# The first refill of the expert ring sent in two transfers behind the first chunk, and output weights laid out by column halves

## The reference

```python
def hier_moe(h, w_rg, b_rg, w_re, b_re, w_gate, w_up, w_down):
    ...
    for e in range(N_EXPERTS):
        hid = jax.nn.silu(t @ w_gate[e]) * (t @ w_up[e])
        out = out + gates[:, e:e + 1] * (hid @ w_down[e]).astype(f32)
```

## Time and profile before

| | |
|---|---|
| median of three runs | 704.38 us (703.09, 704.38, 705.97) |
| profiled execution, its own time | 704.35 us |
| its span, first to last instruction | 702.5 us |
| mean granted TensorE clock | 0.971 of full speed |
| TensorE busy | 636.7 us |
| DMA | 234.09 MB, mean 333 GB/s |
| attention (layer 0's mixer) | about 0 to 155 us |
| experts of layer 0 | about 155 to 355 us |
| gated linear attention | about 355 to 500 us |
| experts of layer 1 | about 500 to 702 us |

### The profile page before, as it was taken

How to read it: one execution, slowest core, us unless ns; L and a number is a source line. 1 busy time by engine, 2 the same in 40 slices (tenths; PEclk the granted TensorE clock), 3 DMA queues, 4 the chain that set the end, 5 groups by cost and what they waited for, 6 DMA issues and landing times.

```text
span 702.5 us, 11653 instructions
## 1 busy us (share of the span) xinstructions
PE 636.7 (91%) x5189; PEld 381.3 (54%) x5189; DVE 234.0 (33%) x509; ACT 130.4 (19%) x287; POOL 44.2 (6%) x69
## 2 busy tenths in 40 slices
PE   7999999999999979959799999999999996778686
PEld 6654875467556635525378544645665552534433
DVE  2137863154332323203145701312723332123122
ACT  2145762111101100100122412222221100001001
POOL 1033100000000000000020600000000000000000
PEclk9999999999999989989999999999999998899899
DMA  9900583739999999999995505559599999999996
GB/s 351 387 37 1 237 363 140 340 120 371 435 428 433 421 437 424 430 433 420 428 424 220 239 1 240 239 221 376 241 383 440 424 420 443 415 437 429 427 423 253
DMA packets 13415, 234.09 MB, mean 333 GB/s; under 512 B 1712, under 2 KB 2864, under 8 KB 3760
## 3 DMA queue, kind: packets, MB, share of 16 engines
q1 hardware_dynamic: 12944, 233.09, 79.1%
q10 hardware_dynamic: 416, 0.18, 0.1%
HBM read 232.22 MB, written 1.05 MB: 332 GB/s over the span
## 4 chain that ended last, share of the span: by engine, by line
PE 62%; DMA 33%; DVE 2%; ACT 1%; issue 1%; SPq 0%; POOL 0%
DMA mem<-in_experts 25%; PE ps L1032 9%; PE ps L717 8%; PE ps L1244 8%; DMA rows<-in_experts 7%; PE ps L781 5%; PE ps L870 4%; PE ps L1235 4%; PE ps L1046 3%; PE ps L1073 3%; PE ps L818 3%; PE ps L808 1%; PE ps L774 1%; DMA mem<-in_mla_w_in 1%; PE ps L890 1%; PE ps L903 1%
## 5 line engine op out<-in xcount | busy, mean ns | idle before, releaser
L1032 PE MATMUL ps<-mem,hT 128*32 128x256 f32 x1824 | 112.4, 400 | 32.7 <-DMA mem<-in_experts 32.6
L1032 PEld LDWEIGHTS ps<-mem,hT 128*32 128x32 f32 x1824 | 60.7, 115 | 84.7 <-DMA mem<-in_experts 39.9
L781 PE MATMUL ps<-mem,rows 128*128 128x128 f32 x512 | 68.0, 292 | 6.3 <-issue 5.0
L781 PEld LDWEIGHTS ps<-mem,rows 128*128 128x128 f32 x512 | 63.2, 203 | 11.2 <-issue 9.5
L717 PE MATMUL ps<-mem,hT 128*128 128x512 f32 x128 | 57.3, 598 | 1.1 <-ACT hT L1592 1.1
L1046 PE MATMUL ps<-mem 128*32 128x512 f32 x464 | 53.1, 595 | 5.4 <-DMA mem<-in_experts 3.4
L1965 DVE TENSOR_TENSOR rows<-rows,ps 128x512 f32<-128x512 f32 x60 | 40.7, 686 | 48.6 <-PE ps L1073 48.4
L1073 PE MATMUL ps<-hT,mem 128*128 128x512 f32 x120 | 55.7, 606 | 0.6 <-ACT hT L1517 0.6
L1244 PE MATMUL ps<-mem,hT 128*128 128x512 f32 x128 | 55.8, 594 | 0.0
L1509 ACT ACTIVATE mem<-ps 128x256 f32<-128x256 f32 x16 | 9.9, 616 | 217.7 <-PE ps L1032 217.7
L1955 DVE TENSOR_TENSOR mem<-mem,ps 128x256 f32<-128x256 f32 x16 | 9.7, 607 | 116.6 <-ACT mem L1509 116.6
(11 more groups left out here) (331 smaller groups left out, 681.6 us busy)
## 6 DMA issues: line engine op xcount, KB each, us to landing
mem<-in_experts SPq DMA_DIRECT2D x31, 4096.0 KB, 33.2
mem<-in_experts SPq DMA_DIRECT2D x25, 2048.0 KB, 22.5
rows<-in_experts SPq DMA_DIRECT2D x9, 2048.0 KB, 29.9
mem<-in_gla_parts SPq DMA_DIRECT2D x3, 4096.0 KB, 27.4
mem<-in_mla_o SPq DMA_DIRECT2D x1, 4096.0 KB, 30.9
mem<-in_gla_parts SPq DMA_DIRECT2D x2, 2048.0 KB, 47.8
mem<-in_mla_w_in SPq DMA_DIRECT2D x2, 1344.0 KB, 9.5
mem<-in_mla_uq SPq DMA_DIRECT2D x1, 2304.0 KB, 15.8
```

Source lines behind the costliest of these rows:

```text
L781: mm = pe.matmul(spot(k), xn[:, i, k, :], Sg[:, i, :], start=first and k % HK == 0, stop=not first, skip_group_check=True)
L1032: mm = pe.matmul(ps[32 * j:32 * j + 32, 2, m * FE:(m + 1) * FE], xe[:, k, 32 * j:32 * j + 32], w[:, j, c * FE:(c + 1) * FE], start=k == 0 ...
```

## The change

Three things are done together.

1. The output weights of both mixers are laid out by column halves, `(b k n)` for `(k n)`: columns 0 to 511 of all chunks, then columns 512 to 1023. Each column half is exactly one place of the ring. In layer 0 half 8 is then issued at out_done 7 and half 9 at out_done 8; in layer 1 half 9 at out_done 11 and half 10 at out_done 12. Part 4 of layer 0 (halves 8 and 9) is thereby two transfers.
2. The gate and up weights of a half are laid out as (chunk, expert, column), so that a quarter of a half is one chunk of all four experts.
3. Half 11 of each layer is sent by `load_first`: its first quarter (512 KB) when TensorE has finished the first chunk of half 0 (signalled by left_done), the other three quarters (1536 KB) when half 0 has been read. Part 5 then counts 48 on its landing semaphore. left_done now counts two per layer, and ACT waits for 2l + 2.

```diff
--- before.py
+++ after.py
@@ -377,13 +377,14 @@
     krT = ring[:, o_cq + 5 * POS:o_cq + 6 * POS]
     sqk = heads(ring[:, o_cq:o_cq + HEADS * NOPE])
     assert o_sq + QW <= o_q and o_cq + 6 * POS <= 2 * PART
-    wmo, wv, wrr, wgo = (SLOT[i].rearrange("p (k n) -> p k n", k=KD) for i in (2, 1, 2, 0))
+    wv, wrr = (SLOT[i].rearrange("p (k n) -> p k n", k=KD) for i in (1, 2))
+    wmo, wgo = (SLOT[i].rearrange("p (b k n) -> p b k n", b=2, k=KD) for i in (2, 0))
     PARTS = 3 * GROUPS
     NHALF = [2 * NSLOT + 1, 2 * NSLOT + 1]
     FIRST = [7, 2]
     HALVES = [mem[:, i * HALF:(i + 1) * HALF] for i in range(2 * NSLOT)] + [extra]
     wgq, wgk = (r.rearrange("p (k n) -> p k n", k=KD) for r in HALVES[0:2])
-    WHALF = [r.rearrange("p (e n) -> p e n", e=GE) for r in HALVES]
+    WHALF = [r.rearrange("p (c e n) -> p e c n", c=HK, e=GE) for r in HALVES]
     DHALF = [r.rearrange("p (e k n) -> p e k n", e=GE, k=2) for r in HALVES]
     EARLY = 8
     RING = 6
@@ -402,10 +403,12 @@
     def split(l, p):
 
         first, second = place(l, 2 * p), place(l, 2 * p + 1)
-        return 2 * p + 1 >= NHALF[l] and p < EARLY or p == PARTS - 1 or second != first + 1 or second == 2 * NSLOT or p == PARTS - 2
+        return 2 * p + 1 >= NHALF[l] and p < EARLY or p == PARTS - 1 or second != first + 1 or second == 2 * NSLOT or p == PARTS - 2 or (l, p) == (0, 4)
 
     def signalled(l, p):
 
+        if p == NHALF[l] // 2:
+            return 48
         return 32 if split(l, p) and p < PARTS - 2 else 16
 
     def landing(l, p):
@@ -498,7 +501,7 @@
             for r in range(MASK_ROWS):
                 sp.dma_start(t[QK + r:QK + r + 1, :, :],
                              a["mask_rows"][m, r:r + 1].unsqueeze(1).to_broadcast([1, HEADS, POS])).then_inc(in_rows, 16)
-        sp.dma_start(wmo, a["mla_o"].rearrange("p (k n) -> p k n", k=KD)).then_inc(w_out, 16)
+        sp.dma_start(SLOT[2], a["mla_o"]).then_inc(w_out, 16)
         sp.dma_start(late[:, :], a["late"]).then_inc(in_moe, 16)
 
         def source(l, g, t):
@@ -513,6 +516,15 @@
             p, m = divmod(q, 2)
             done = {2 * PARTS - 4: up_landed, 2 * PARTS - 2: half_landed}.get(q, landing(l, p)[0])
             sp.dma_start(HALVES[place(l, q)], source(l, p // 3, p % 3)[:, m * HALF:(m + 1) * HALF]).then_inc(done, 16)
+
+        def load_first(l, q):
+
+            p, m = divmod(q, 2)
+            src, dst = source(l, p // 3, p % 3)[:, m * HALF:(m + 1) * HALF], HALVES[place(l, q)]
+            sp.wait_ge(left_done, 2 * l + 1)
+            sp.dma_start(dst[:, 0:HALF // HK], src[:, 0:HALF // HK]).then_inc(landing(l, p)[0], 16)
+            sp.wait_ge(FAST.read, read_by(l, q - NHALF[l]))
+            sp.dma_start(dst[:, HALF // HK:], src[:, HALF // HK:]).then_inc(landing(l, p)[0], 16)
 
         def load_part(l, p):
 
@@ -533,7 +545,9 @@
             for p in range(done // 2, PARTS):
                 if split(l, p):
                     for q in (2 * p, 2 * p + 1):
-                        if q >= done:
+                        if q == NHALF[l]:
+                            load_first(l, q)
+                        elif q >= done:
                             sp.wait_ge(FAST.read, read_by(l, q - NHALF[l]))
                             load_half(l, q)
                 else:
@@ -553,7 +567,7 @@
 
         sp.wait_ge(k_sums, 3)
         turned = (a_job, len(AJOBS))
-        experts(0, [((3, 4, 5, 6, 7), turned), ((0, 1, 2, 10), (o_copied, HEADS // 2)), ((8, 9), (out_done, 8))])
+        experts(0, [((3, 4, 5, 6, 7), turned), ((0, 1, 2, 10), (o_copied, HEADS // 2)), ((8,), (out_done, 7)), ((9,), (out_done, 8))])
         for q, half, done in ((37, 0, w_gq), (38, 1, w_gk)):
             sp.wait_ge(FAST.read, read_by(0, q))
             sp.dma_start(HALVES[half], a["gla_parts"][0, :, half * HALF:(half + 1) * HALF]).then_inc(done, 16)
@@ -567,7 +581,7 @@
         sp.dma_start(SLOT[0], a["gla_parts"][3]).then_inc(w_out, 16)
 
         experts(1, [((0, 1), (g_job, V_END)), ((4, 5), (g_att, 2)), ((2, 3), (g_job, R_END)),
-                    ((6, 7, 8), (g_yT, 2)), ((9, 10), (out_done, 12))])
+                    ((6, 7, 8), (g_yT, 2)), ((9,), (out_done, 11)), ((10,), (out_done, 12))])
         for b, cols in enumerate((slice(0, 512), slice(512, 512 + QC), slice(512 + QC, D))):
             for i in range(2):
                 sp.wait_ge(FAST.add, LAST_ADD[1] + NT[1] * b + i + 1)
@@ -715,7 +729,7 @@
                             pe.wait_ge(*HALF_ADDED[l])
                             logits_turned(ORDER[n][:-1])
                         mm = pe.matmul(ps[:, OUT[l][2 * i + b], :], hT[:, k, META + i * P:META + (i + 1) * P],
-                                       w[:, k, b * 512:(b + 1) * 512], start=k == 0, stop=k == KD - 1)
+                                       w[:, b, k, :], start=k == 0, stop=k == KD - 1)
                     mm.then_inc(out_done, 1)
 
             early = ORDER[n][:-1]
@@ -805,8 +819,9 @@
 
             for n, k in enumerate(ks):
                 for j in range(4):
-                    mm = pe.matmul(ps[QUAD * j:QUAD * (j + 1), bank, 0:width], src[:, k, 0:QUAD],
-                                   w[:, n, j * width:(j + 1) * width], start=n == 0, stop=n == len(ks) - 1)
+                    cols = w[:, n, j * width:(j + 1) * width] if len(w.shape) == 3 else \
+                        w[:, j // 2, n, (j % 2) * width:(j % 2 + 1) * width]
+                    mm = pe.matmul(ps[QUAD * j:QUAD * (j + 1), bank, 0:width], src[:, k, 0:QUAD], cols, start=n == 0, stop=n == len(ks) - 1)
             return mm
 
         def mla():
@@ -1016,7 +1031,7 @@
                     mm = pe.transpose(ps[:, 4, COL[i]:COL[i] + R], Gg[0:R, i, :], ident[0:R, 0:R])
                 mm.then_inc(K.turn, 1)
 
-            def expand(K, n, m, halves, waits=(), first=0):
+            def expand(K, n, m, halves, waits=(), first=0, opens=False):
 
                 for b, w in enumerate(halves):
                     if b < first:
@@ -1030,8 +1045,10 @@
                         for j in range(GE):
 
                             mm = pe.matmul(ps[32 * j:32 * j + 32, 2, m * FE:(m + 1) * FE],
-                                           xe[:, k, 32 * j:32 * j + 32], w[:, j, c * FE:(c + 1) * FE],
+                                           xe[:, k, 32 * j:32 * j + 32], w[:, j, c, :],
                                            start=k == 0 and m == 0, stop=k == KD - 1, skip_group_check=True)
+                        if opens and k == 0:
+                            mm.then_inc(left_done, 1)
                     mm.then_inc(K.read, 1)
 
             def hidden_turned(K, n):
@@ -1102,7 +1119,7 @@
             pe.wait_ge(FAST.send, 2 * n0 + 1)
             for b in range(2):
                 rows_gathered(1, range(HK * b, HK * (b + 1)), False).then_inc(FAST.rows, 1)
-            expand(FAST, n0, 0, part(0))
+            expand(FAST, n0, 0, part(0), opens=True)
             pe.wait_ge(FAST.send, 2 * n0 + 2)
             gates_turned(FAST)
             expand(FAST, n0, 1, part(1))
@@ -1527,7 +1544,7 @@
                         act.wait_ge(FAST.comb, COMB0[l] + NA[l] * g)
                     gates_copied(FAST, n0 + g + 1, GT[(g + 1) % 2])
                 half_out(FAST, n0 + g)
-            act.wait_ge(left_done, l + 1)
+            act.wait_ge(left_done, 2 * l + 2)
             act.copy(ysb[:, 512:512 + QC], ps[:, 6, 0:QC]).then_inc(left_kept, 1)
             with act.If(over_):
                 with act.Fori(0, ROUNDS) as r:
@@ -2127,9 +2144,12 @@
         full[:NOPE, 0] = col[:NOPE]
         return full
 
+    def by_columns(w):
+        return w.reshape(KD, P, 2, D // 2).transpose(1, 2, 0, 3).reshape(P, -1)
+
     def parts(w):
         w = w.reshape(2, GROUPS, GE, 2, HK, P, w.shape[3])
-        return w.transpose(0, 1, 5, 3, 2, 4, 6).reshape(2, GROUPS, P, -1)
+        return w.transpose(0, 1, 5, 3, 4, 2, 6).reshape(2, GROUPS, P, -1)
 
     def halves(w):
         w = w.reshape(2, GROUPS, GE, P, 2, 2, D // 2).transpose(0, 1, 3, 5, 2, 4, 6)
@@ -2140,8 +2160,8 @@
     w = x["gla_w_in"][0]
     vo, ro = 2 * GH * GDK, 2 * GH * GDK + GH * GDV + GRANK
     out["gla_parts"] = np.stack([np.concatenate([by_block(w[:, 0:vo // 2]), by_block(w[:, vo // 2:vo])], 1), by_block(w[:, vo:ro - GRANK]), by_block(w[:, ro:]),
-                                 by_block(x["gla_w_o"][0])])
-    out["mla_o"] = by_block(x["mla_w_o"][0])
+                                 by_columns(x["gla_w_o"][0])])
+    out["mla_o"] = by_columns(x["mla_w_o"][0])
     out["mla_w_in"] = by_block(x["mla_w_in"][0])
     out["gains"] = np.stack([x["norm_mix"][0], x["norm_ffn"][0], x["norm_mix"][1], x["norm_ffn"][1]])\
         .reshape(4, KD, P).transpose(2, 0, 1)
```

## The result

The changed kernel takes 706.88 us (median of 20 runs, 702.58 to 711.66), the kernel before 703.95 (20 runs, 702.58 to 706.51): ratio 1.0036, 95% interval 1.002 to 1.0051. That is 2.9 us slower by the medians, where 2.4 us faster was forecast. By the bound named ahead of the result, 0.5%, it counts as no change, yet it lies above the stated range, 700.3 to 704.8, and the interval excludes a gain.

A forecast was written before the change was run, and what follows sets the result against it. Both layers were taken to end when their stream of expert weights has landed. From 704.35 us, 1.22 us per layer for the opening (2.44 in all), everything else zero, gave 701.9 us; range 700.3 to 704.8.

The forecast's parts named there:

- The issue times: SP queue: half 8 near 144.3, half 9 near 490.6, the 512 KB quarter near 162.7 and 508.6 us.
- The column halves: Output weights: halves 8 and 9 issued about 7.4 us earlier, data moved into the early rest, worth nothing by itself.
- The stages between the layers and behind the last product: Attention, gated and store stages behind each layer keep their lengths; a tail longer than 6.7 us would be wrong.
- the one on the opening: Start of each layer's stream: a quarter of half 11 moves inside the rest, saving 1.22 us per layer, 2.44 in all.
- if the quarter's own start-up is paid twice: Lower bound of the saving at each stream's start: in this case the saving is nothing.
- if the engine that lands last does not rest there: Other condition of the lower bound at each stream's start: the saving is nothing.
- the rival that buys nothing: Stream start: the quarter only queues on the slowest of 16 engines, or the signal comes hardly earlier; 704.35 us, chance 0.11.
- Transfers start in series: Stream start: the second part starts only when the first has landed; 0.9 us late per layer, 706.2 us, chance 0.06.
- the prediction's sum by a fixed cost: Quarter of half 11: with about 2.0 us fixed per DMA it would take 3.2 us instead of 1.22.
- The clock falls before the tail: Layer tails: TensorE at 1.2 GHz doubles the work behind the last landing; 709.6 us, one layer 705.8; chance 0.05 together.
- The start-up loss is saved too: Stream start: the quarter also takes the slow start's loss into the rest; 3.4 us saved, 701.0 us, chance 0.12.

The follow-up runs named there:

- two chunks opened: Changed kernel with half 11 sent as 1024 KB behind the second chunk and 1024 KB behind the reading of half 0: 703.36 us, ratio 0.9996 to the kernel before.
- three chunks: Changed kernel with half 11 sent as 1536 KB behind the third chunk and 512 KB behind the reading of half 0: 704.52 us, ratio 0.9991.
- with the tails filled: More unread transposes in the last group's three waits (20, 10, 8 for 12, 4, 2): kernel before 703.82 us, ratio 0.9986; changed kernel 706.79 us, 1.0025.
- the cut alone: Changed kernel with both parts of half 11 (512 and 1536 KB) issued behind the reading of half 0, nothing earlier: 705.42 us, ratio 1.0015.
- the opening in steps: Changed kernel with half 11 as 512 KB behind the first chunk, 512 KB behind the second, 1024 KB behind the reading: 705.37 us, ratio 1.0012.

## Why the prediction was wrong

**What held.** Both layers end with the landing of their stream, and what the stream gains or loses at its start is found at its end: two chunks opened give 0.85 us per layer for a lead of 0.86 us, three chunks 0.33 for 0.43. The issue times came within 0.1 to 0.5 us of the forecast. The column halves were worth nothing, as the rest hides them. The stages between the layers and behind the last product kept their lengths, 158.2 and 6.7 us in every profile.

**The step that failed** is the one on the opening: "The rest of half 11 starts moving at 165.0 and 510.75 as now, with 0.524 MB less ahead of the end. Saving: 1.22 us per layer". The remainder's first packet is at 165.78 in layer 0 and 511.90 in layer 1, and 7 and 12 of its packets take over 1 us where 0.46 is usual. By the packets finished, the changed kernel is 0.5 MB ahead at 4 us behind the first expand, 0.18 MB at 6 us, and not at all at 8 us (about 1.8 MB in both, layer 0). The term is -1.22 in the text and +0.94 us per layer by the mean of eight intervals, +1.9 us in all. That mean is not the whole of the 2.9 us between the medians, but within the interval of the ratio, 1.4 to 3.6 us.

**The bound that was missing.** I named the case "if the quarter's own start-up is paid twice" and bounded the term below by nothing for it, without a sum. The rows had a price for a start: 0.35 to 0.58 us, from 414 and 404 GB/s in the first ten microseconds. By that price the term would have been -0.64 to -0.87 us instead of -1.22, still a gain. Measured over the eight layers with this opening, the second start took 9.6 to 17.1 us of packet time, 0.6 to 1.1 us for each of 16 engines by division. That takes away most of the saving. It doesn't make a loss of it.

**Where the loss comes from.** The semaphore records hold 16 completions for each transfer, which I take as one for each engine. Those of the next-to-last half, in us behind the first expand, as means:

```
                             mean of the 16    14th of 16    last
no opening (6 layers)             180.80          182.41     182.80
512 + 1536 KB (8 layers)          181.03          182.29     183.74
1024 + 1024 KB (6 layers)         180.10          181.76     181.94
```

On the average of its completions the changed stream is only 0.23 us late, and its 14th is level. In seven of the eight layers the last two or three completions come 1.4 to 1.8 us behind the others; in the kernels without an opening the last six or seven come within a microsecond, with no such gap. The layer waits for the last. The eighth layer has no straggler (last three at 181.81, 181.89 and 182.08): it is the interval of 182.22 that stands apart in the table. Already the last packet of half 11 ends late: at 9.75 to 10.70 us with this opening, at 8.70 to 9.01 without, at 8.02 to 8.57 with two chunks. The prediction had named this engine too, in the bound ("if the engine that lands last does not rest there") and in the rival that buys nothing, but as a saving lost, not as a loss.

**The rivals.** *Transfers start in series* gave 0.9 us late per layer and 706.2 us, with a chance of 0.06. Its number was near; its mechanism was not: the remainder doesn't wait for the quarter's landing (its packets begin at 3.61 us, the quarter's end at 4.47), so the number was in part luck. The quarter took 4.3 and 3.9 us from issue to landing, where the prediction's sum by a fixed cost had 3.2 us. The Trainium skill, DMA: Bandwidth & Descriptors, "Rules for kernel authors", asks for at least 1 MiB per DMA; here 1024 KB gains and 512 KB loses, so the trace agrees for a first part on an idle queue. Behind a full queue little is left of the rule: each extra transfer of 512 KB cost 0.06 to 0.09 us there. *The clock falls before the tail* happened in this profile, for 1.03 and 1.08 us rather than 3.85 a tail, since only part of the tail is at 1.2 GHz. But it falls in other kernels too, without an opening as well, and with the tails filled the difference is as large: it belongs to single profiles, not to the difference. *The start-up loss is saved too* has the two-chunk opening for it and the quarter against it: the longer lead lost and the shorter one gained.

**What stays open.** Why two or three of 16 completions fall behind and stay behind for 180 us is not shown: the packet records don't name the engine. Half 11's late last packet doesn't settle it: the layer without a straggler had it (9.75 us), and one layer of the cut alone had it too (11.30 us, with a packet of 1.90 us) and ended at 183.23. Nor is it known why the opening in steps pays a second start.

## What to carry to other kernels

When a transfer is cut so that its first part may start in a rest, the first part must be long enough to cover the start of the second; in this kernel 1024 KB sent 0.86 us ahead did and 512 KB sent 1.3 us ahead did not, and the earlier issue of the small part made the whole later. Price a cut by the packets of the part behind it and by the last of the 16 completions, not their average, and let the bound reach below zero. In a kernel whose tail is a chain of short waits, filling the waits to the end is worth a try: it lengthened nothing on the path here, and the clock stayed full in all six tails.

## What was not expected of the hardware

Issue to landing for the last 1536 KB of a half was longer (8.2 and 8.3 us) than for all of its 2048 KB (7.2 and 7.7 us), with the same issue point; what had changed was the 512 KB issued 1.3 us earlier. Transfers of 512 KB behind a full queue cost only 0.06 to 0.09 us each. Two or three late completions of 16 kept a layer waiting for over a microsecond. And the granted clock fell in 9 of 22 layer tails with waits of 0.9 to 1.7 us between short products and in none of 6 with waits of 0.2 to 0.6 us.
